# Five of eight K pairs per group by seven products, with a ring of seven slots in that stage

## What is computed

```
def swiglu(h, w_gate, w_up, w_down):
    return (jax.nn.silu(h @ w_gate) * (h @ w_up)) @ w_down
```

```
def implicit_filters(feat, t, w1, b1, fr1, w2, b2, fr2, w3):
    h = jnp.sin(f32(fr1) * (feat @ f32(w1) + f32(b1)))
    h = jnp.sin(f32(fr2) * (h @ f32(w2) + f32(b2)))
    h = h @ f32(w3)
    ...
    return h[:, :D_HYENA] * decay, h[:, D_HYENA:] * decay
```

## Time and profile before

| | us |
|---|---|
| median of three runs | 2572.56 (2571.4 to 2573.23) |
| the profiled execution | 2573.23 |
| its span, first to last instruction | 2571.4 |
| TensorE busy | 2561.0 (100%) |
| VectorE busy | 2017.4 (78%) |
| ScalarE busy | 1507.8 (59%) |

### The profile page before, as it was taken

How to read it: one execution, slowest core, us unless ns; L and a number is a source line. 1 busy time by engine, 2 the same in 40 slices (tenths; PEclk the granted TensorE clock), 3 DMA queues, 4 the chain that set the end, 5 groups by cost and what they waited for, 6 DMA issues and landing times.

```text
span 2571.4 us, 36476 instructions
## 1 busy us (share of the span) xinstructions
PE 2561.0 (100%) x14027; PEld 2207.6 (86%) x14027; DVE 2017.4 (78%) x2927; ACT 1507.8 (59%) x2221; POOL 328.7 (13%) x292
## 2 busy tenths in 40 slices
PE   9999999999999999999999999999999999999998
PEld 8888888888889888888888888888888888888887
DVE  7787777777977878899888998887876767666675
ACT  6666658776656555555555566445654545455554
POOL 2111103316201001111111152101100000000000
PEclk9999999999999999999999999999999999999999
DMA  7565666565656556666566556556566666665664
GB/s 246 182 221 182 191 201 197 174 204 196 206 176 199 169 180 197 197 196 197 195 196 194 194 180 222 155 172 197 188 197 190 190 193 189 193 191 190 191 191 159
DMA packets 137351, 493.67 MB, mean 192 GB/s; under 512 B 15447, under 2 KB 16344, under 8 KB 136792
## 3 DMA queue, kind: packets, MB, share of 16 engines
q1 hardware_dynamic: 136600, 490.80, 60.5%
q10 hardware_dynamic: 576, 0.53, 0.1%
HBM read 489.14 MB, written 2.13 MB: 191 GB/s over the span
## 4 chain that ended last, share of the span: by engine, by line
PE 98%; DVE 1%; ACT 1%; issue 0%; DMA 0%; ACTq 0%
PE ps L1180 46%; PE ps L1177 23%; PE ps L1096 5%; PE ps L1098 5%; PE ps L1097 5%; PE ps L1150 4%; PE ps L1152 4%; PE ps L1151 4%; PE ps L1194 1%; DVE wl L1835 1%; PE ps L1320 0%; PE ps L1165 0%; PE ps L1166 0%; PE ps L1167 0%; ACT wh L1437 0%; ACT T L1437 0%
## 5 line engine op out<-in xcount | busy, mean ns | idle before, releaser
L1835 DVE TENSOR_TENSOR wl<-raw,wh 128x1024 fp32r<-128x1024 f32 (+2 forms) x908 | 1119.6, 1241 | 389.0 <-ACT wh L1437 388.0
L1437 ACT ACTIVATE wh<-raw 128x1024 fp32r<-128x1024 f32 (+2 forms) x908 | 938.5, 1039 | 635.9 <-PE ps L1177 391.6
L1180 PE MATMUL ps<-X,wh 128*128 128x512 f32 x3600 | 1204.9, 395 | 0.8 <-DVE X L1841 0.8
L1177 PE MATMUL ps<-X,wl 128*128 128x256 f32 x3600 | 904.3, 278 | 0.0
L1180 PEld LDWEIGHTS ps<-X,wh 128*128 128x128 f32 x3600 | 652.3, 188 | 127.9 <-issue 2.3
L1177 PEld LDWEIGHTS ps<-X,wl 128*128 128x128 f32 x3600 | 660.7, 188 | 31.2
L1180 PE MATMUL ps<-XG,wh 128*128 128x512 f32 x1472 | 491.6, 395 | 1.3 <-DVE hT L1835 1.3
L1177 PE MATMUL ps<-XG,wl 128*128 128x256 f32 x1472 | 366.8, 278 | 0.0
L1180 PEld LDWEIGHTS ps<-XG,wh 128*128 128x128 f32 x1472 | 265.3, 188 | 51.9 <-DVE hT L1835 1.6
L1177 PEld LDWEIGHTS ps<-XG,wl 128*128 128x128 f32 x1472 | 269.7, 188 | 14.2
L1437 ACT ACTIVATE T<-ps 128x256 f32<-128x256 f32 (+1 forms) x380 | 126.6, 383 | 192.9 <-PE ps L1177 192.2
(11 more groups left out here) (257 smaller groups left out, 2467.9 us busy)
## 6 DMA issues: line engine op xcount, KB each, us to landing
raw<-in_w_down SPq DMA_DIRECT2D x176, 512.0 KB, 3.6
raw<-in_w_gu SPq DMA_DIRECT2D x144, 512.0 KB, 3.7
raw<-in_w_gate SPq DMA_DIRECT2D x104, 512.0 KB, 3.5
raw<-in_w_sc SPq DMA_DIRECT2D x95, 512.0 KB, 4.0
raw<-in_w_val SPq DMA_DIRECT2D x88, 512.0 KB, 3.5
raw<-in_w_zx SPq DMA_DIRECT2D x80, 512.0 KB, 3.6
raw<-in_w_in SPq DMA_DIRECT2D x56, 512.0 KB, 3.6
raw<-in_w_osc SPq DMA_DIRECT2D x32, 512.0 KB, 3.7
```

The source lines that it names most:

```text
L1177: t = e.matmul(bank(c, i)[:, 0:256], wl[:, b0:b0 + 128], X[:, kx * 512:kx * 512 + 256], start=False, stop=sp and kk == c.kn - 1)
L1180: e.matmul(bank(c, i)[:, :], wh[:, b0:b0 + 128], X[:, kx * 512:kx * 512 + 512], start=st and kk == 0, stop=False)
L1437: return e.activation(out, in_, ACT.Copy, scale=scale)
L1835: return e.tensor_tensor(out, a, b, op)
```

## The change

The default pattern becomes "SCSSCSSC" and that of group 3 "CCSSCSSC": five S pairs in place of four in groups 4 to 10, four in place of three in group 3. NS becomes 5. From group 3 to the end of the first FFN, `ring()` gives units seven slots in place of four: the three new ones lie in XM at word 7168 and up. To make room, the piece spill copies the filters (KS, fml, fmh, 2 MB) to a DRAM tensor during group 2, and bload copies them back; their users wait for it (d_back). The operands Sx move to the start of XM, over the filters, so sb0 waits until the copy is done (d_spill). Splits are put up to six steps ahead in that stage, and sb0 to sb2 begin one step earlier, with one round more. Their scratch is now in Ts, which lies under the tiles of gsilu1 and gprod, so gsilu1 of group 2 waits for the last of sb2.

```diff
-PATTERN = {2: "CCCCCCCC", 3: "CCSCSCSC"}
+PATTERN = {2: "CCCCCCCC", 3: "CCSSCSSC"}
+USUAL = "SCSSCSSC"
 NG = 9
-NS = 4
+NS = 5
...
+U_DEEP = [GROUPS[1].first, [c for c in COLS if c.kind == "rn" and c.ph == 3][0].first]
+NDEEP = 3
+
+def ring():
+    order, slots, before, last = list(range(NW)), [], [], {}
+    for u in range(NU):
+        if u == U_DEEP[0]:
+            order = list(range(NW, NW + NDEEP)) + order
+        if u == U_DEEP[1]:
+            order = [r for r in order if r < NW]
+        r = order.pop(0)
+        order.append(r)
+        slots.append(r)
+        before.append(last.get(r))
+        last[r] = u
+    return slots, before
...
+    put(GROUPS[0].first + 5, "spill", 0)
+    put(GROUPS[0].first + 6, "spill", 1)
     for j in range(NS):
-        s = GROUPS[0].first + 7 + 2 * j
+        s = GROUPS[0].first + 6 + 2 * j
...
+                if piece == "spill":
+                    w.wait_ge(fV, 35)
+                    w.wait_ge(fl, 6)
+                    w.wait_ge(fsA, 3)
+                    w.wait_ge(fsV, 3)
+                    if i:
+                        e.dma_start(spilled[:, 3584:4096], fmh.bitcast(F32)).then_inc(d_spill, 16)
+                    else:
+                        e.dma_start(spilled[:, 0:3072], a_(0, 3072)).then_inc(d_spill, 16)
+                        e.dma_start(spilled[:, 3072:3584], fml.bitcast(F32)).then_inc(d_spill, 16)
...
                     for dst, name in ((IF, "dftI"), (ws, "gm_ws"), (bs, "gm_bs"), (wp, "pool_w"), (gain2, "gm_gb")):
                         e.dma_start(dst, T_[name]).then_inc(d_b2, 16)
+                    w.wait_ge(d_spill, 128)
+                    e.dma_start(a_(0, 3072), spilled[:, 0:3072]).then_inc(d_back, 16)
+                    e.dma_start(fml.bitcast(F32), spilled[:, 3072:3584]).then_inc(d_back, 16)
+                    e.dma_start(fmh.bitcast(F32), spilled[:, 3584:4096]).then_inc(d_back, 16)
...
-                    if i >= NW:
-                        w.wait_ge(mm, i - NW + 1)
-                    copy(parted(wh, i), source(i)).then_inc(hi, 1)
+                    if WBEFORE[i] is not None:
+                        w.wait_ge(mm, WBEFORE[i] + 1)
+                    if WSLOT[i] >= NW:
+                        w.wait_ge(d_spill, 128)
+                    copy(parted(0, i), source(i)).then_inc(hi, 1)
...
                 if piece == "sb0":
+                    w.wait_ge(d_spill, 128)
...
                         if not U_SUM[i.i]:
                             w.wait_ge(mm, i.last + 1)
                             w.wait_ge(gT, GT + 2 * (i.i - 2))
                             w.wait_ge(pl, 8)
                             w.wait_ge(nrs, 4)
+                            w.wait_ge(sbA, SBA + 3 * NS)
+                            w.wait_ge(sbV, SBV + 5 * NS)
```

More of the change, by code:

```diff
@@ L323, in schedule @@
         put(-1, "split0", k)
[L324 to L328, removed]
-        if part(u) == "b":
-            put(u - 3, "tc", u)
-            put(u - 2, "td", u)
+    step = 0
+    for u in range(2, NU):
+        if u < 7:
+            step = (0, 1, 2, 3, 3)[u - 2]
+        elif WBEFORE[u] is None:
+            step = max(step, u - 3 - (u - U_DEEP[0] + 1) // 2)
+        else:
+            step = max(step, WBEFORE[u] + 1)
+        if U_DEEP[0] <= u < U_DEEP[1]:
+            step = max(step, U_DEEP[0] - 3 + (u - U_DEEP[0]) // 2)
+        put(step, "split", u)
+        if part(u) == "b":
+            put(step, "tc", u)
+        if part(u) == "a":
+            put(step, "td", u - 1)
+    put(GROUPS[0].first + 5, "spill", 0)
+    put(GROUPS[0].first + 6, "spill", 1)
     for j in range(NS):
-        s = GROUPS[0].first + 7 + 2 * j
+        s = GROUPS[0].first + 6 + 2 * j
         if j:
@@ L792, in source, with slot, parted @@
         return raw[:, r * UN + (512 if what == "a" else 0):(r + 1) * UN]
-    def parted(ring, u):
-        b = u % NW
-        return ring[:, b * UN:b * UN + (512 if part(u) == "a" else UN)]
+    def slot(low, u):
+        r = WSLOT[u]
+        if r < NW:
+            return (wl if low else wh)[:, r * UN:(r + 1) * UN]
+        o = 7168 + UN * (r - NW) + NDEEP * UN * low
+        return XM[:, o:o + UN]
+    def parted(low, u):
+        return slot(low, u)[:, 0:512 if part(u) == "a" else UN]
+    spilled = nc.dram_tensor("filters", (128, 4096), F32).ap()
+    d_spill, d_back = d_f1, d_f2
     memT = a_(8192, 4096)
@@ L1094, in group @@
                     xh, xl = (X1[:, 512 * k + p + 128 * h:512 * k + p + 128 * h + 128] for p in (0, 256))
-                W1, W2 = (ring[:, o + 512 * half:o + 512 * half + 512] for ring in (wh, wl))
+                W1, W2 = (slot(low, u)[:, 512 * half:512 * half + 512] for low in range(2))
                 e.matmul(b, xh, W1, start=u == first, stop=False)
@@ L1127, in unit @@
                 w.wait_ge(lo, halves(u))
+            H, L = slot(0, u), slot(1, u)
             st, sp = u == c.first, u == c.last
@@ L1146, in unit @@
                     w.wait_ge(s, n)
-                    b0 = (u % NW) * UN + kk * 512
+                    b0 = kk * 512
                     for i in halves_:
                         xh, xl = (X[:, kx * 512 + o + 128 * i:kx * 512 + o + 128 * i + 128] for o in (0, 256))
-                        e.matmul(bank(c, i)[:, :], xh, wh[:, b0:b0 + 512], start=not goes and st and kk == 0, stop=False)
-                        e.matmul(bank(c, i)[:, :], xh, wl[:, b0:b0 + 512], start=False, stop=False)
-                        t = e.matmul(bank(c, i)[:, :], xl, wh[:, b0:b0 + 512], start=False,
+                        e.matmul(bank(c, i)[:, :], xh, H[:, b0:b0 + 512], start=not goes and st and kk == 0, stop=False)
+                        e.matmul(bank(c, i)[:, :], xh, L[:, b0:b0 + 512], start=False, stop=False)
+                        t = e.matmul(bank(c, i)[:, :], xl, H[:, b0:b0 + 512], start=False,
                                      stop=sp and kk == c.kn - 1 and (not goes or c.kind == "on"))
@@ L1174, in unit @@
                     w.wait_ge(s, n)
[L1175 removed]
+                    b0 = kk * c.w + 128 * i
                     if low:
[L1177 removed]
+                        t = e.matmul(bank(c, i)[:, 0:256], L[:, b0:b0 + 128], X[:, kx * 512:kx * 512 + 256], start=False,
                                      stop=sp and kk == c.kn - 1)
                     else:
[L1180 removed]
+                        e.matmul(bank(c, i)[:, :], H[:, b0:b0 + 128], X[:, kx * 512:kx * 512 + 512], start=st and kk == 0,
                                  stop=False)
@@ L1876, in vector @@
                 if piece == "sb1":
-                    A11, A21, A12, A22 = (Tc[:, 128 * n:128 * n + 128] for n in range(4))
-                    S1, S2, S3, S4 = (Tc[:, 512 + 128 * n:640 + 128 * n] for n in range(4))
+                    A11, A21, A12, A22 = (Ts[:, 128 * n:128 * n + 128] for n in range(4))
+                    S1, S2, S3, S4 = (Ts[:, 512 + 128 * n:640 + 128 * n] for n in range(4))
                     w.wait_ge(sbA, SBA + 3 * i + 2)
```

40 lines of the change are left out of this document (21 added, 19 removed).

## The result

The changed kernel takes **2620.62 us** (median of four runs, 2619.97 to 2623.49) against 2572.57 before: 48 us more, a ratio of 1.0189 with a 95% interval of 1.0172 to 1.0207. The forecast was 2578.6 us in a range of 2571 to 2587. The sign was right; of the size, the two copies explain only a part (e4 has them alone, at 8 us).

What follows compares the result with a forecast made beforehand. TensorE, busy 100% of the span, was taken as the bound. -4.7 - 2.2 + 8.3 + 4.6 = +6.0 us, with 0 for VectorE, on the median 2572.56 gave 2578.6 us, range 2571 to 2587.

Steps and rivals of the forecast that it cites:

- S pairs, -4.7 and -2.2: TensorE in the groups: eight more S pairs save 0.59 us each (-4.7); seven first S pairs lose their 0.32 wait (-2.2).
- VectorE in the groups, 0 (range 0 to 7): VectorE's extra 4.1 us per period still fits, at 97%, costing 0; range allows 1 us in each of seven periods.
- 0.9 us to spare: At the first sum of products (gsum0) behind a group: VectorE needs 39.8 us against 40.7 on TensorE.
- VectorE becomes the bound: Rival in the groups: POOL, late raw tiles or ScalarE waits cost 1 us a period, giving 2585.6 us; chance 15%.
- Entry, +8.3: Group 2: ScalarE and VectorE wait for the filters' copy out, so the first S pair runs 8.3 us late.
- Leaving, +4.6: Next phase's norm: the weight load queues behind the filters' copies back, making TensorE's transposes 4.6 us late.
- copies beside the loads: Rival at entry and leaving: copies use time loads leave free; return costs nothing, entry 6.2 or less, 2565.7 to 2571.9; 18%.
- The clock's fall: Rival at the transposes' and norm's stalls: TensorE falls to half clock, 1.9 us each, giving 2580.5 or 2582.4; chance 15%.
- The missing saving: Rival: an S pair right behind another runs as long as a plain one, adding 4.7 us, giving 2583.3; chance 2%.

Runs made afterwards that it cites:

- e4: The kernel before (four pairs, four slots) with only the filters' copies to DRAM and back and the waits on them; 2580.46 us.
- e5: Changed kernel with splits of w_down units, the last sixteen excepted, three units ahead, four from the sixth ordinary unit behind a group on; 2590.73 us.
- e9: e8 with seven slots from ten units into group 2, scalings spread further, splits three ahead behind group 10, borders left free; 2571.02 us (0.9995).
- e2: Changed kernel with the patterns of before (four S pairs a group), keeping the seven slots and both copies; 2597.36 us.
- e7: Changed kernel with the filters returning in five pieces, three units apart, from eight units behind the old place on; 2614.26 us.
- e8: Changed kernel with e5's split order, e7's return in pieces, and scalings of operands later, into a buffer over the next phase's zero borders; 2579.2 us.
- e1: Changed kernel with splits of ordinary w_down units behind a group at most three units ahead, not six; 2601.23 us.

## Why the prediction was wrong, point by point

**S pairs, -4.7 and -2.2: right, with one cost left out.** A period without waits is 64.14 us (e5), against 63.8 forecast. The difference is in the new slots: a plain unit from the slots in XM takes 2.80 us where one from most slots of wh and wl takes 2.72, an ordinary one 2.82 against 2.78 (medians of the distances of starts in e5). Why was not tried; 0.08 us on six plain and 0.04 on eight ordinary units, three slots in seven, make the 0.34. So the change can save 388.27 - 384.77 = 3.5 us in six periods (before, and e9) and not 5.5. The kernel before over its six periods:

```profile
1038.21:1426.48 388.27, 387.94 (x1899) 324.23 (x1898) 348.31 (x385) 219.35 (x270) 44.08 (x48) 1.00 0.61 195
```

**VectorE in the groups, 0 (range 0 to 7): the step that failed.** "0.9 us to spare" before the first sum was 2.2 short. In group 6 VectorE needed 43.0 us from the group's start to the end of the first addition, not 39.8: the four S pairs took 1.2 us more than 25.6 (6.6 us each, and 0.6 for one split that ran beside POOL), the last ordinary unit's addition into hT (0.75) was not counted, and waits came to 4.1 and not 3.3. Each is small; against 0.9 us they decide: 2.0 to 2.9 us of waiting a period, 14.5 in six. The second failing is that I checked the first sum alone. What stands behind it, gsum2 to gprod and the transposes, has its own wait of up to 1.5 us in each period, 6.7 in six, and e2 shows that this one needs no fifth pair. With the clock's falls the six periods came out at +23.6 us and not -5.5. The rival "VectorE becomes the bound" named the right place, and late raw tiles with it, but priced it at 1 us a period and took VectorE's time for the cause. It was the order: e5 does the same work in 64.1 us. The five splits that I counted ahead of the first sum as given were the removable part; before the change two stood there. Whether more raw slots, with the deep order left as it is, would have ended the burst's waits was not tried.

**Entry, +8.3: the cause was right, the split among the places was not, and the clock came on top.** The copy was seen by ScalarE at 936.4; with the 2.0 us that this run lost earlier, the forecast was 935.0. What was missing is seen in the rows: the DMA engines move 389 GB/s until 934.4, then nearly nothing, and the copy counts as done 1.9 us later. The Trainium skill (DMA: Bandwidth & Descriptors, Anatomy of one DMA — SWDGE (gpsimd) path) says of a DMA issued by GpSimd that its semaphore can't be raised until the last byte is confirmed as landed, and gives some 2.0 us of fixed cost, most of it for that. This copy is issued by SP; its 1.9 us are near that figure, and no run here shows what they consist of. At the first S pair the kernel was 11.2 us late: 6.0 of waiting, 3.8 ahead of unit 316, 2.2 ahead of the transposes and none ahead of the first a unit (8.3 forecast, as 2.5, 4.2 and 1.6), and most of the rest half clock: unit 316 alone took 5.29 us and not 2.72. So that 8.3 is not further from 11.2 is in part luck, waits forecast too long against a clock left out. That the copy's wait is not absorbed because the deeper order uses up the slack is borne out by e4 and e2: 1.4 us with four slots and 7.0 with seven, both with four pairs, though e2 also has the change's order of the scalings.

**Leaving, +4.6: right, and the clock on top.** The load behind the copies landed 11.8 us after issue (13 forecast), 3.9 us more than before; counted from the last of the five constants it was also issued 1.7 us later, behind the copies' own issues. That makes 5.6 us, where 5.4 was forecast, and the norm's transposes waited 4.61 us. Behind them the clock was 0.61 on average for 4.4 us, some 1.7 us, which is the rest of 6.4. The rival of copies beside the loads needed this load less than 0.8 us later than before; e7, where the copies stand elsewhere on the queue, shows that it is the queue's order.

**The clock's fall was a rival and came true**, priced at 1.9 us a stall for two stalls. That price was read from the start of the trace, where the rows show a clock of 1.00 in both stretches; what a fall costs is first shown here, 1.7 us at the norm. The granted clock went to half behind both stalls at the entry, behind the one at the norm, and behind three of the seven groups' waits. By an estimate from the rows here and above, length of a row times the clock that is missing, this cost some 11 us in all:

```profile
1095.00:1100.00 5.00, 3.89 (x14) 3.35 (x15) 4.97 (x7) 1.65 (x2) 0.00 (x0) 0.66 0.92 239
1440.00:1445.00 5.00, 5.00 (x22) 4.31 (x21) 4.79 (x7) 1.34 (x2) 0.00 (x0) 0.66 0.80 240
1508.00:1513.00 5.00, 5.00 (x21) 4.35 (x21) 5.00 (x8) 1.77 (x4) 0.00 (x0) 0.66 0.78 282
```

The Trainium skill (TensorE: Matmul & The Clock Gate, What's actually happening) states that the throttled clock is the default and that activity releases it. The trace agrees in that each of these falls stands behind a wait; but four groups' waits of much the same length (2.0 to 2.9 us) were not followed by a fall, nor was one of 3.2 us at the entry of e7, so a fall can't be told from a wait's length alone.

**Not forecast at all:** the end of the ring, behind group 10 (2.8 us, and 3.7 against the saving). In the changed kernel most of it is the first sum's wait again (2.0 us); where that is gone, in e5 and e8, two waits for sums into hT (1.0 and 1.8 us) stand in its place, behind splits that the way back from seven slots to four puts ahead of them. They are gone in e1 and e9, where splits stay three steps ahead up to the next phase. **The missing saving** did not come to pass.

## What to carry to other kernels

A deeper ring is not free when one in-order queue serves both the ring and the evacuations: each slot lets another load-dependent split stand ahead of a sum that frees banks. So when a change deepens a ring, list what now stands ahead of each evacuation, and hold the pieces that need no depth where they were. And "it fits at 97%" holds only for the best order; with less than 1 us to spare at one place, look at the place behind it as well.

## What the runs showed of the hardware

**A split beside POOL's additions into hT takes mostly 1.8 us and not 1.22.** VectorE and POOL in the first period's end, in the changed kernel:

```profile
1191.25 1.44 POOL L2534 TENSOR_TENSOR hT<-hT,T 128x256 f32<-128x256 f32 x2 [4.21 <-DVE hT L1901]
```
```profile
1191.98 1.79 DVE L1901 TENSOR_TENSOR XM<-raw,XM 128x1024 fp32r<-128x1024 f32 x1 [0.48 <-ACT XM L1497]
```

In e5 the 732 splits of a raw tile that overlap no POOL instruction take 1.16 to 1.23 us; of 75 that overlap these additions 62 take 1.5 us or more, up to 1.81. The Trainium skill (SBUF — State Buffer, SBUF: two separate sides) has a VectorE instruction with two SBUF inputs and a GpSimd one that reads SBUF shut each other out of a shared port for a whole instruction. The trace agrees in that such splits are longer; which of the two waited it doesn't show. The kernel before has 50 such long splits, and my 1.14 us left them out.

**The start varies by up to 3 us.** From 10 to 14 us the changed kernel's profiled run has 14 matmuls and the kernel before 24, with no change in that part of the program:

```profile
10.00:14.00 4.00, 4.00 (x14) 3.35 (x13) 3.08 (x7) 3.42 (x7) 0.00 (x0) 1.00 0.97 358
```
```profile
10.00:14.00 4.00, 4.00 (x24) 3.48 (x24) 2.95 (x6) 3.41 (x6) 0.00 (x0) 1.00 1.03 399
```

Single profiled runs must be compared from a common point, not from the span's start.
